# Second mixer, first pair of latent heads: two weight chunks split ahead of softmax steps and copies, three filling banks emptied first

## The reference

```
u = rmsnorm(x) @ w_in
xc, gb, gc, cq, ckv, kr, glog = split(u)
y_conv = (gb * short_conv(gc * xc)) @ w_conv_out
q = rmsnorm(cq) @ w_uq ;  kv = rmsnorm(ckv) @ w_ukv          # 8 latent heads, 128 + 64 wide
p = softmax((q_nope k_nope^T + q_rope k_rope^T) * scale)     # per head, 256 x 256
y_mla = (p v, heads side by side) @ w_mla_out
x = x + (sigmoid(glog_conv) * y_conv + sigmoid(glog_mla) * y_mla) @ w_mix_out
```

## Time and profile before

| | us |
|---|---|
| median of 3 runs | 1658.27 (1657.46 to 1659.21) |
| the profiled execution's own time | 1661.43 |
| its span in the profile | 1659.6 |
| PE busy | 1335.3 (80%) |
| DVE busy | 575.2 (35%) |
| ACT busy | 418.3 (25%) |

### The profile page before, as it was taken

How to read it: one execution, slowest core, us unless ns; L and a number is a source line. 1 busy time by engine, 2 the same in 40 slices (tenths; PEclk the granted TensorE clock), 3 DMA queues, 4 the chain that set the end, 5 groups by cost and what they waited for, 6 DMA issues and landing times.

```text
span 1659.6 us, 23159 instructions
## 1 busy us (share of the span) xinstructions
PE 1335.3 (80%) x9160; PEld 858.9 (52%) x9160; DVE 575.2 (35%) x1233; ACT 418.3 (25%) x640; POOL 69.0 (4%) x140
## 2 busy tenths in 40 slices
PE   6899998989986977977989899999775655556556
PEld 5588898754543433533668798999511112112112
DVE  4433676544332322331373575573300001001001
ACT  4334675201111111101063444453210000000002
POOL 3910000000000000000000000000000000000000
PEclk9899999999998988988999999999798878888777
DMA  9977525869999999999954244445799999999995
GB/s 316 285 241 277 190 103 200 350 246 414 382 379 423 397 404 422 404 404 422 366 182 153 102 153 153 153 162 227 312 419 413 420 417 414 421 416 416 422 415 213
DMA packets 126136, 523.10 MB, mean 315 GB/s; under 512 B 12440, under 2 KB 16688, under 8 KB 84592
## 3 DMA queue, kind: packets, MB, share of 16 engines
q1 hardware_dynamic: 121344, 518.68, 79.1%
q0 software_dynamic: 4576, 2.95, 0.8%
q10 hardware_dynamic: 144, 0.44, 0.1%
HBM read 520.96 MB, written 1.06 MB: 315 GB/s over the span
## 4 chain that ended last, share of the span: by engine, by line
PE 54%; DMA 19%; SPq 19%; DVE 4%; issue 3%; ACT 2%; DVEq 0%; ACTq 0%; PEldq 0%
PE psum L1885 19%; DMA ring<-in_w_up_e_dram 10%; SPq L584 10%; PE psum L2268 9%; SPq L588 8%; PE psum L2241 4%; DMA ring<-in_w_exp_up_dram 3%; PE psum L2313 3%; PE psum L1898 2%; DMA ring<-in_w_mem_kv_dram 2%; DMA ring<-in_w_exp_down_dram 2%; DVE ring_r L1051 2%; PE psum L2230 1%; PE psum L2549 1%; PE psum L2097 1%
## 5 line engine op out<-in xcount | busy, mean ns | idle before, releaser
L1885 PE MATMUL psum<-arena_r,ring_r 128*128 128x256 f32 x2784 | 348.0, 285 | 24.0 <-DVE arena_r L1096 6.4
L1885 PEld LDWEIGHTS psum<-arena_r,ring_r 128*128 128x128 f32 x2784 | 337.8, 192 | 35.5 <-issue 14.9
L2268 PE MATMUL psum<-ring,arena 128*32 128x512 f32 (+1 forms) x1152 | 188.8, 639 | 68.5 <-DMA ring<-in_w_up_e_dram 67.7
L1051 DVE TENSOR_TENSOR ring_r<-ring,ring_r 128x1024 fp32r<-128x1024 f32 x156 | 181.6, 1220 | 143.7 <-ACT ring_r L682 142.8
L682 ACT ACTIVATE ring_r<-ring 128x1024 fp32r<-128x1024 f32 x156 | 153.0, 1049 | 75.4 <-DMA ring<-in_w_in_dram 33.0
L2685 PE MATMUL psum<-ring,arena 128*32 128x512 f32 x752 | 114.5, 749 | 65.8 <-DMA ring<-in_w_exp_up_dram 63.5
L2268 PEld LDWEIGHTS psum<-ring,arena 128*32 128x32 f32 (+1 forms) x1152 | 56.7, 128 | 183.7 <-issue 122.3
L2703 PE MATMUL psum<-ring,arena 128*32 128x512 f32 x384 | 66.5, 827 | 49.5 <-DMA ring<-in_w_exp_down_dram 46.5
L2685 PEld LDWEIGHTS psum<-ring,arena 128*32 128x32 f32 x752 | 23.8, 124 | 148.5 <-DMA ring<-in_w_exp_up_dram 100.3
L2313 PE MATMUL psum<-ring,arena 128*32 128x512 f32 (+1 forms) x576 | 92.9, 609 | 3.2 <-DVE arena L1470 2.2
L1829 DVE TENSOR_TENSOR arena<-arena,psum 128x256 f32<-128x256 f32 x16 | 6.7, 421 | 254.3 <-ACT arena L1009 254.3
(11 more groups left out here) (403 smaller groups left out, 1367.7 us busy)
## 6 DMA issues: line engine op xcount, KB each, us to landing
ring<-in_w_gate_e_dram SPq DMA_DIRECT2D x64, 1024.0 KB, 12.7
ring<-in_w_up_e_dram SPq DMA_DIRECT2D x64, 1024.0 KB, 14.8
ring<-in_w_down_e_dram SPq DMA_DIRECT2D x64, 1024.0 KB, 16.3
ring<-in_w_exp_down_dram SPq DMA_DIRECT2D x96, 512.0 KB, 15.5
ring<-in_w_exp_gate_dram SPq DMA_DIRECT2D x47, 1024.0 KB, 25.9
ring<-in_w_exp_up_dram SPq DMA_DIRECT2D x47, 1024.0 KB, 26.3
ring<-in_w_in_dram SPq DMA_DIRECT2D x20, 2048.0 KB, 9.0
ring<-in_w_ada_dram SPq DMA_DIRECT2D x12, 2048.0 KB, 13.2
```

Source lines behind the costliest of these rows:

```text
L1051: V.tensor_tensor(lo, whole, hi.bitcast(F32), ALU.subtract).then_inc(w_low, 1)
L1885: ins = product(lambda a_, b_, k, first, last: mm(ps[:, t * T:(t + 1) * T], a_[:, k, c], b_[:, k, :], start=first, stop=last), w, x, arriving)
L2268: ins = mm(psum[c, 5, :], xg1[:, k, P * j + width * b:P * j + width * (b + 1)], gate[e][:, :, k, :], start=(k == 0), stop=(k == KT - 1))
```

## The change

For p = 0 alone. On ACT, the whole of chunk kb+4 is rounded ahead of the two heads' exponentials, where it was rounded behind them. The whole of chunk kb+5 is rounded right behind them, where its two halves stood between the copies. On DVE, the low part of kb+4 is made ahead of the row maxima, where it stood behind the division; and the banks of `fill0`, `fill1` and `fill2` are emptied ahead of the low part of kb+5, where that of `fill2` was emptied behind it. Pairs 1 to 3 keep their order.

```
# ACT
 for p in range(HEADS // 2):
     h0, h1 = 2 * p, 2 * p + 1
+    if p == 0:
+        high(kb + 4)
     latent_exp(h0)
     latent_exp(h1)
-    high(kb + 4 + h0)
+    high(kb + 5 if p == 0 else kb + 4 + h0)
     copy_out(f"lp{h0}", at_pT[0])
-    high(kb + 4 + h1, (0, 1))
+    if p:
+        high(kb + 4 + h1, (0, 1))
     copy_out(f"lp{h1}", at_pT[1])
     copy_out(f"lo{h0}", oT[:, h0, :], full(act, f"lo{h0}")[:, 0:T])
-    high(kb + 4 + h1, (2, 3))
+    if p:
+        high(kb + 4 + h1, (2, 3))
     copy_out(f"lo{h1}", oT[:, h1, :], full(act, f"lo{h1}")[:, 0:T])
# DVE
     pair = (2 * p, 2 * p + 1)
+    if p == 0:
+        low_part(kb + 4)
     for s in pair:
         softmax_max(f"ls{s}", s, (MLA_NOPE + MLA_ROPE) ** -0.5)
     for s in pair:
         softmax_norm(f"ls{s}", s)
-    low_part(kb + 4 + 2 * p)
+    if p:
+        low_part(kb + 4 + 2 * p)
     fill_out(4 * p)
     fill_out(4 * p + 1)
+    if p == 0:
+        fill_out(2)
     low_part(kb + 5 + 2 * p)
-    fill_out(4 * p + 2)
+    if p:
+        fill_out(4 * p + 2)
     fill_out(4 * p + 3)
```

## The result

The changed kernel takes 1647.3 us by the median of 4 runs (1645.62 to 1649.01), against 1658.74 before: 11.4 us less, ratio 0.9931 with a 95% interval of 0.9915 to 0.9946 (9.0 to 14.1 us). Run again in another session it gave 1648.45 (6 runs), ratio 0.9937 [0.9925, 0.9950].

What follows compares the result with a forecast made beforehand. PE, with 54% of the chain, bounds the kernel, idle at two waits in pair 0. Gains 2.53 + 3.64 + 1.57 = 7.7 us, or 9.3 with a second clock loss; 8.5 taken from 1658.27 gives 1649.8, range 1647.8 to 1653.8.

Steps and rivals of the forecast that it cites:

- step 1: At fill2 in pair 0: splitting kb+4 early removes 2.53 of the 2.83 us wait, with 4.8 us to spare.
- step 4: On ACT: kb+5, landed by 903.7, is rounded at 916.8 to 920.7 and does not hold up the copy.
- step 5: On DVE: banks emptied first, low part of kb+5 at 925.8 to 930.4, 6 us ahead of PE's need.
- step 6: On PE: scores of pair 1 start at 933.8 instead of 941.52; all 3.64 us of the second wait go.
- step 2: Softmax of pair 0: maxima taken 0.9 us late, at no cost because fill1 and fill2 cover it.
- step 3: ACT's rounding beside DVE's rotary step: no slowing counted; a possible 0.3 us lies inside 0.69 us of slack.
- Nothing taken back in the experts: Behind the stage: PE itself releases later loads, so the experts' first loads start earlier by the same 7 to 8 us.
- step 7: PE's granted clock: 1.57 us comes back at fill2; a loss of the same size possible at the second gap.
- The clock gives nothing back: Rival: slow stretch belongs to place or time and is found elsewhere; gain 6.2 us, 1652.1; chance 0.13.
- only one wait goes: Rival: PE stops at fill4 instead, or the first wait stays; 4.1 or 3.64 us left, 1654.2 to 1654.6; chance 0.07.
- taken back in the experts: Rival: expert loads from 1200 us on have their own start, so no gain comes out; 1658.3; chance 0.05.
- slower: Rival: a late chunk kb+4 holds up softmax as well as fill2; 1659 and more; chance 0.03.

Runs made afterwards that it cites:

- experiment 1: Kernel before with only chunk kb+4 split ahead of the softmax of pair 0: 1655.58 us (12 runs), ratio 0.9984.
- experiment 2: Kernel before with only kb+5 rounded right behind the exponentials and fill2's bank emptied ahead of its low part: 1650.12 us (10 runs), ratio 0.9964.
- experiment 11: Kernel before with only DVE's emptying of fill2's bank moved ahead of the low part of kb+5: 1656.58 us (12 runs), ratio 0.9977.
- experiment 12: Kernel before with only ACT's rounding of kb+5 moved right behind the exponentials, in one piece: 1651.25 us (6 runs), ratio 0.9950.
- experiment 4: Changed kernel with 6 matmuls of constants in the wait ahead of conv0: 1647.37 us (6 runs), ratio 0.9938.
- experiment 10: Kernel before with 7 matmuls of constants in the second wait alone: 1659.86 us (11 runs), ratio 1.0003.
- experiment 13: Changed kernel with 3 matmuls of constants (about 1.3 us) added ahead of the scores of pair 1: 1651.27 us (6 runs), ratio 0.9952.
- experiment 3: Kernel before with 9, 13 and 6 matmuls of constants in the three waits, overfilling them: 1659.6 us (12 runs), ratio 1.0003.
- experiment 14: Changed kernel with 6 matmuls of constants (about 2.6 us) added ahead of the scores of pair 1: 1650.71 us (5 runs), ratio 0.9946.
- experiment 16: Kernel before with 5 matmuls of constants in the first wait alone: 1658.82 us (11 runs), ratio 1.0001.
- experiment 5: Kernel before with 5, 7 and 3 matmuls of constants in the three waits, within their length: 1655.44 us (11 runs), ratio 0.9979.
- experiment 8: Changed kernel with ACT rounding the first half of conv's input ahead of its last head-output copy: 1645.0 us (5 runs), ratio 0.9918.
- experiment 7: Kernel before run again unchanged, for a second profile: 1658.46 us (11 runs), ratio 1.0001; the profiled execution took 1653.38 us.

## Why the prediction was right and where it was wrong

**The two waits (steps 1, 4, 5, 6): right, to 0.2 us.** PE's times in relation to the scores of pair 0 came out as reckoned: `fill2` 9.06 us behind them (reckoned 9.06), the scores of pair 1 23.5 (23.7). The 2.53 and 3.64 us are confirmed apart (experiments 1, 2, 11, 12). What the prediction did not see is that either of the two moves of the second half alone takes that wait away. (Of DVE's differences only the four of kb+4 change place, not eight; the sum does not use that count.)

**The delay of softmax and the rounding beside the rotary step (steps 2, 3): right.** The maxima came 0.9 us late and PE did not wait for them; the rotary step kept its pace.

**Nothing taken back in the experts: right in the main.** Their first load was issued at 1122.14, against 1133.34 before, 11.2 us earlier; the last products start 10.6 us earlier (1631.85 against 1642.48), so 0.6 us of it was lost in between. Between first load and last products the 18 profiles have 507.6 to 509.8 us, the repeat of before 508.1 and the three of the changed kernel (experiment 4 among them) 509.7 to 509.8; a loss of that size, up to 1.7 us, can't be told from scatter. The first load in the profile after:

```profile
1122.14 0.34 SPq L584 DMA_DIRECT2D ring<-in_w_exp_gate_dram  x1
```

**The clock (step 7): the step that failed.** I took 1.57 us behind the first wait, which is what came back (7.42 against 5.84 us), and half of another loss behind the second, about 2.3 us together. The measured gain of 10.4 to 11.4 us (by the two ratios) less 6.2 us of waits leaves 4 to 5 us. The half loss behind the second wait was not there (experiment 10); instead 1.5 us came back at `conv0` and 1.8 in the last stage, for which the sum had no term. Three errors stand behind that:

- *The later places were taken as fixed.* I wrote that the 1.81 us wait at `conv0` stays, which is so, and left its clock loss standing with it. Of the 10.8 us between the two profiles behind the first scores, 7.9 lie up to the scores of pair 1, 0.2 up to those of pair 2, 1.5 at `conv0` and 1.8 in the last stage; the experts take back 0.6. (The 1.3 us that the prediction read at `conv0` was 1.5: unslowed, the 96 matmuls take 11.44 us and not two times 5.85.) Of the 18 profiles, four have both falls (before, experiments 10, 11, 13), three have one (3, 14, 16) and eleven none, the three of the changed kernel (with experiment 4) among these; in 3, 4 and 5 the wait at `conv0` was filled and in 8 there was none.
- *The loss was tied to one wait.* It is not: fill the first wait and the second pays (experiment 16), fill the second and the first goes on paying (10); fill all three and 3.5 us come back (5). The two waits are worth more together than apart: up to the scores of pair 2, 8.1 us against 1.4 + 4.0. The whole times are too coarse to show it (2.7 and 6.0 us by the ratios, 3.6 and 9.0 by the medians).
- *The range ended at a loss at two places.* Its low end, 1647.8, had that and about 1 us of room. `conv0` stood in the earlier trace rows as a third place, with 1.3 us; the measured time lies inside a range that has it.

**From the profiles to the medians, by an estimate.** Each profile is one execution. But the code ahead of pair 0 is the same in all kernels, and a kernel's median less the span of its profile behind the first scores (so what lies ahead of the scores, and the little that a time has beyond its span) comes to 908.3 to 910.6 us in 17 of the 18 (before 1658.74 - 749.5 = 909.2, after 1647.3 - 738.7 = 908.6). The exception is experiment 7, with 913.7, whose profiled execution was the fastest of its 11. So the typical execution of before seems to pay at both later places, and that of the change at neither. That the change loses these falls because it moves the places is the reading that fits; the run with 1.3 us added, where they are back, and experiments 11 and 12 speak for it. It is argued, not shown.

**The rivals.** "The clock gives nothing back" is refuted by experiment 5 and by `fill2` in the profile after, "only one wait goes", "taken back in the experts" and "slower" by the profile after. What stays open is why the clock falls at `conv0` in one execution of before and not in another, why it falls there in one kernel's profile and not in another's, and, beyond the estimate above, how much of the median difference each later place holds.

## What to carry to other kernels

Where splits or casts of weights stand behind a step whose input is late, while the weights are long there, put them ahead; what decides is that each engine's new wait ends before the next engine needs its result, and here there were 6 us of room. When PE's waits are ended, price the clock as a thing of the whole kernel: a loss behind one wait can move to the next when only that one goes (1.6 us in experiment 16, 2.7 in experiment 1), and places far behind may have a stretch at 1.2 GHz in one version and not in the other. A forecast for a kernel like this should list every place with such a stretch in the profile of before, here 1.5 to 1.8 us each, and carry each in its range, touched or not.

## What the runs showed of the hardware that was not expected

- The length of a wait doesn't tell whether the clock falls behind it: 1.81 us ahead of `conv0` had a fall behind it in 6 of 14 profiles, 3.64 us had none in both profiles of the kernel before, and with the first wait gone or filled the same 3.64 us had a loss of almost 3 us (experiment 1) and of 1.6 us (16). The section "HAM oscillation — how this bites in real kernels" of the page TensorE: Matmul & The Clock Gate (the Trainium skill) warns that PE, stalled between bursts of matmuls, drops back and starts the next burst cold. Its example has waits for DMA of about 3 to 5 us. The rows agree in kind, with falls of the clock behind waits, but not in size: here falls came behind breaks of 2.83 and 1.81 us.
- The fall behind the first wait was no matter of chance: all six profiles that have this wait unfilled (before, its repeat, experiments 2, 10, 11, 12) have it, with `fill2` at 7.42 to 7.45 us each time. Those at `conv0` and in the last stage varied, between the two profiles of before too.
- Executions differ by up to 6.5 us already at the end of the first block's experts (820.4 to 827.0 us over the 18 profiles, 3.5 between the two of before), with the same code up to there. The whole spans of one profile each can't tell a gain of that size from chance; a stage must be compared from its own start.
